# Norm sums between the groups of a projection, and one pass over x at the entry to a second network

## The reference

```
# first network, per layer l (cut)
u = rms_norm(x, g_mix[l]) * (1 + sc_a) + sh_a          # "stat_mix": mean of x*x
...
x = x + gt_a * (merged @ w_out[l])                     # "w_out0".."w_out7"
u = rms_norm(x, g_ffn[l]) * (1 + sc_f) + sh_f          # "stat_ffn"
h = silu(u @ w_ffn_gate[l]) * (u @ w_ffn_up[l])
x = x + gt_f * (h @ w_ffn_down[l])                     # "down0".."down7"
# after two layers
x = rms_norm(x, g_final)                               # "norm0"
# second network, first layer
h_lat = modulate(rmsnorm(x,   norm_g[0, 0]), sh1, sc1)     # "norm1", both together
h_ctx = modulate(rmsnorm(ctx, norm_g[0, 0]), csh1, csc1)
```

## Time and profile before

| | |
|---|---|
| median of 3 runs | 2476.86 us (2463.89 to 2481.15) |
| the profiled execution | 2472.51 us, its span 2470.7 us |
| TensorE busy | 2227.5 us, 90% of the span |
| DVE busy | 1634.2 us, 66% |
| ACT busy | 1174.1 us, 48% |
| mean granted TensorE clock | 0.949 of 2.4 GHz |
| matmuls of the sums, L913 and L1064 | 84 records, 144 records |

### The profile page before, as it was taken

One profiled execution on the slowest core, in us unless ns is written; L12 is line 12 of the kernel. 1 busy time (PEld: TensorE's weight loads), 2 busy tenths in 40 slices (PEclk: granted clock), 3 DMA queues, 4 the chain that ended last, 5 costly groups with the idle time before them and its releaser, 6 DMA issues.

```text
span 2470.7 us, 36391 instructions
## 1 busy us (share of the span) xinstructions
PE 2227.5 (90%) x13724; PEld 1945.1 (79%) x13724; DVE 1634.2 (66%) x2617; ACT 1174.1 (48%) x2021; POOL 32.4 (1%) x18
## 2 busy tenths in 40 slices
PE   1899988999899998999786989989998899898998
PEld 0897778999897788999575566768775788888998
DVE  5557766984458776984477588938584723575983
ACT  3345563563445564563434634435253324644772
POOL 4000000000000000000000000000000000000000
PEclk8899998999899998999898999989999899998999
DMA  6456633865456633865352063535351323313553
GB/s 257 137 179 235 211 101 120 263 231 180 136 178 235 210 111 120 268 226 182 117 178 104 3 202 128 179 106 183 121 179 60 128 94 111 103 52 128 187 179 113
DMA packets 107181, 385.08 MB, mean 156 GB/s; under 512 B 11664, under 2 KB 16272, under 8 KB 105744
## 3 DMA queue, kind: packets, MB, share of 16 engines
q1 hardware_dynamic: 75680, 272.66, 32.8%
q10 hardware_dynamic: 31344, 110.24, 12.8%
HBM read 381.81 MB, written 1.05 MB: 155 GB/s over the span
## 4 chain that ended last, share of the span: by engine, by line
PE 70%; DVE 15%; DMA 6%; ACT 5%; issue 3%; ACTq 1%; DVEq 0%; SPq 0%
PE ps L863 18%; PE ps L867 18%; PE ps L866 18%; DVE ada_junk L1776 6%; DMA ring<-tape_in 3%; DMA work<-adas_in 3%; PE ps L880 3%; PE ps L884 3%; PE ps L883 3%; DVE ring_l L1751 2%; PE ps L1064 1%; PE ps L1199 1%; DVE part L1751 1%; ACT ring_r L1240 1%; PE ps L1149 1%
## 5 line engine op out<-in xcount | busy, mean ns | idle before, releaser
L863 PE MATMUL ps<-part,ring_l 128*128 128x256 f32 (+1 forms) x3808 | 1188.1, 312 | 100.2 <-DVE part L1861 39.1
L867 PE MATMUL ps<-part,ring_r 128*128 128x256 f32 (+1 forms) x3808 | 1171.5, 308 | 0.0
L866 PE MATMUL ps<-part,ring_r 128*128 128x256 f32 (+1 forms) x3808 | 1170.6, 307 | 0.0
L863 PEld LDWEIGHTS ps<-part,ring_l 128*128 128x128 f32 x3808 | 731.5, 192 | 163.1 <-issue 73.7
L1240 ACT ACTIVATE ring_r<-ring 128x1024 fp32r<-128x1024 f32 x511 | 535.4, 1057 | 633.3 <-DMA ring<-tape_in 520.3
L1751 DVE TENSOR_TENSOR ring_l<-ring,ring_r 128x1024 fp32r<-128x1024 f32 x511 | 616.0, 1220 | 221.8 <-ACT ring_r L1240 219.4
L866 PEld LDWEIGHTS ps<-part,ring_r 128*128 128x128 f32 x3808 | 733.8, 193 | 31.6
L867 PEld LDWEIGHTS ps<-part,ring_r 128*128 128x128 f32 x3808 | 731.7, 192 | 33.1
L1776 DVE SCALAR_TENSOR_TENSOR ada_junk<-work 128x1024 bf16<-128x1024 f32 x272 | 345.6, 1270 | 45.6 <-DMA work<-adas_in 30.1
L880 PE MATMUL ps<-ring_l,part 128*128 128x512 f32 x264 | 106.1, 402 | 11.0 <-ACT work L1588 6.2
L883 PE MATMUL ps<-ring_r,part 128*128 128x512 f32 x264 | 105.9, 401 | 0.0
(11 more groups left out here) (198 smaller groups left out, 1798.0 us busy)
## 6 DMA issues: line engine op xcount, KB each, us to landing
ring<-tape_in SPq DMA_DIRECT2D x518, 512.0 KB, 3.4
work<-adas_in ACTq DMA_DIRECT2D x176, 512.0 KB, 4.3
work<-ada_first_in ACTq DMA_DIRECT2D x8, 1024.0 KB, 16.2
work<-bias_in ACTq DMA_DIRECT2D x1, 2048.0 KB, 9.8
work<-cond_in ACTq DMA_DIRECT2D x1, 1536.0 KB, 8.0
x<-x_t_in ACTq DMA_DIRECT2D x1, 1024.0 KB, 12.8
x<-ctx_in ACTq DMA_DIRECT2D x1, 1024.0 KB, 5.6
x<-dist_in ACTq DMA_DIRECT2D x1, 1024.0 KB, 7.4
```

The lines of the kernel that those rows point to most:

```text
L863: mm = pe.matmul(dst, lhsT=wl, rhs=mr, start=(k == 0), stop=False)
L866: pe.matmul(dst, lhsT=wr, rhs=mr, start=False, stop=False)
L867: mm = pe.matmul(dst, lhsT=wr, rhs=ml, start=False, stop=(k == len(moving) - 1))
```

## The change

1. In the first network the squares and sums of stat_ffn are taken tile by tile: ACT squares tile k once DVE has made it, and TensorE's sum matmul for tile k stands behind group k + 2 of w_out. So five of the eight stand between groups, three behind the last. The same is done with stat_mix of layer 1 between the down groups of layer 0. ACT's rounding for the last group (`finished("w_out7")`, `finished("down7")`) moves behind the logarithm and exponential.
2. In the last layer the down groups carry the sums for the second network. ACT squares each tile twice, as x² and as (g·x)² with g = g_final, and TensorE sums both in one matmul of 512 columns (`stat_last`). The context is loaded in the feed-forward stage of that layer, squared ahead of the down groups and summed behind down1 (`stat_ctx`).
3. The scale of norm1 for `x` is worked out from these sums without a pass over the normed `x`: with s = mean x² + eps, DVE multiplies 1/s by the sum of (g·x)² (`lat_power`), and ACT takes logarithm and exponential again ("norm1x"). Norm0's scaling of `x` (`final`) is interleaved with norm1's scaling on DVE, two tiles ahead.
4. The modulation and gains of the second network's first norm are made before the down groups.

```diff
@@ TensorE, first network
+                def stat_part(k):
+                    dst = bank("stat_mix")[:, 0:T]
+                    pe.wait_ge(*squared(k, l + 1))
+                    mm = pe.matmul(dst, lhsT=const("ones"), rhs=sq[:, k, :], start=(k == 0), stop=(k == KD - 1))
...
+                def stat_last(k):
+                    pe.wait_ge(*squared2(KD + k))
+                    mm = pe.matmul(bank2("norm0"), lhsT=const("ones"), rhs=SQ_OF[0][:, k, :, :].rearrange("p a t -> p (a t)"),
+                                   start=(k == 0), stop=(k == KD - 1))
...
                 for f in range(KD):
                     project(f"w_out{f}", pairs(mix_r, mix_l, KD), (lambda k: mix_made(k, l)) if f == 0 else None)
-                stat("stat_ffn", [(squared, KD + k, sq[:, k, :]) for k in range(KD)])
+                    if f >= LAG:
+                        stat_mixed(f - LAG)
+                for f in range(KD - LAG, KD):
+                    stat_mixed(f)
...
                 for f in range(KD):
                     project(f"down{f}", pairs(hidden_r, hidden_l, FT), (lambda k: hidden_made(k, l)) if f == 0 else None)
+                    if l == DEPTH - 1 and f == 1:
+                        for k in range(KD):
+                            stat_ctx(k)
+                    if f >= LAG:
+                        (stat_part if l < DEPTH - 1 else stat_last)(f - LAG)
+                for f in range(KD - LAG, KD):
+                    (stat_part if l < DEPTH - 1 else stat_last)(f)
...
-            stat2("norm0", squared2, 0, SQ_OF[0], T)
-            stat2("norm1", squared2, 1, SQ_OF[1], T2)
@@ ACT
                 for k in range(KD):
-                    finished(f"w_out{k}")
                     act.wait_ge(*x_mixed(k, l))
                     act.activation(sq[:, k, :], xt[:, k, :], ACT.Square).then_inc(squared.sem, 1)
-                inverse_rms(3, "stat_ffn", D)
+                    if k < KD - 1:
+                        finished(f"w_out{k}")
+                inverse_rms(3, "stat_ffn", D, l)
+                finished(f"w_out{KD - 1}")
                 shifted(1, 3)
...
+                    if l == DEPTH - 1 and f == FT // 2:
+                        act.wait_ge(*u_made(2 * KD - 1, l))
+                        act.dma_start(x[:, :, T:T2], ctx_in).then_inc(loaded["ctx"], 16)
...
+                    for f in range(KD):
+                        act.wait_ge(*x_ready(f, DEPTH))
+                        act.activation(SQ_OF[0][:, f, 0, :], xt[:, f, :], ACT.Square)
+                        act.activation(SQ_OF[0][:, f, 1, :], xt[:, f, :], ACT.Square,
+                                       scale=misc_of("g_final")[:, f:f + 1]).then_inc(squared2.sem, 1)
+                        if f < KD - 1:
+                            finished(f"down{f}")
...
+                    act.wait_ge(*done2("norm0"))
+                    act.activation(lat_log, bank2("norm0")[:, 0:T], ACT.Ln, scale=1.0 / D, bias=const("eps")).then_inc(log_mean2.sem, 1)
+                    act.wait_ge(*log_mean2(ROOT["norm0"]))
+                    act.activation(lat_inv, lat_log, ACT.Exp, scale=-1.0).then_inc(rstd2_made.sem, 1)
+                    act.activation(lat_rstd, lat_log, ACT.Exp, scale=-0.5).then_inc(rstd2_made.sem, 1)
+                    act.wait_ge(*lat_power(0))
+                    act.activation(rstd2[:, 0:T], lat_inv, ACT.Ln, scale=1.0 / D, bias=const("eps")).then_inc(log_mean2.sem, 1)
+                    act.wait_ge(*log_mean2(ROOT["norm1x"]))
+                    act.activation(rstd2[:, 0:T], rstd2[:, 0:T], ACT.Exp, scale=-0.5).then_inc(rstd2_made.sem, 1)
+                    finished(f"down{KD - 1}")
...
             act.wait_ge(*x_ready(KD - 1, DEPTH))
-            act.dma_start(x[:, :, T:T2], ctx_in).then_inc(loaded["ctx"], 16)
             act.dma_start(na_bias, bias_in).then_inc(loaded["na"], 16)
...
-            norm_in(0, lambda k: x_ready(k, DEPTH), None)
-            act.wait_ge(loaded["ctx"], 16)
-            norm_in(1, lambda k: scaled2(k), 0)
+            shifted2(1, 0)
@@ DVE, entry to the second network
+            dve.wait_ge(*rstd2_made(ROOT_MADE["norm0"]))
+            dve.tensor_tensor(lat_inv, lat_inv, bank2("norm0")[:, T:T2], ALU.mult).then_inc(lat_power.sem, 1)
+            dve.wait_ge(*rstd2_made(ROOT_MADE["norm0_root"]))
+            for k in range(LAG):
+                final(k)
+            dve.wait_ge(loaded["ctx"], 16)
             norm_in(1, 0, 0)
```

More of the change, by code:

```diff
@@ L312, in ffn @@
         return o + [f"post{1 + 2 * j}"]
-    o = ["norm0", "norm1"] + [f"sgu_g{b}" for b in range(4)] + [f"na_qk{f}" for f in range(2 * WT)]
+    o = ["norm1", "norm0"] + [f"sgu_g{b}" for b in range(4)] + [f"na_qk{f}" for f in range(2 * WT)]
     o += [f"sgu_u{f}" for f in range(WT)] + [f"mix{t}" for t in range(WT)] + [f"na_v{b}" for b in range(4)]
@@ L764, in bank2 @@
         def bank2(name):
-            return ps[:, GROUP2[name] % BANKS]
+            return ps[:, {"norm0": STAT_BANK, "norm1": CTX_BANK}.get(name, GROUP2[name] % BANKS)]
         def done2(name):
@@ L1309, in load_ada @@
                         .then_inc(ada_landed[t % ADA_SLOTS], 16)
[L1311 to L1314 removed]
+                if l == 0:
+                    for k in range(KD):
+                        act.wait_ge(*x_ready(k))
+                        act.activation(sq[:, k, :], xt[:, k, :], ACT.Square).then_inc(squared.sem, 1)
+                    inverse_rms(0, "stat_mix", D, l)
                 shifted(0, 0)
@@ L1820, in _, with modulation2, gain2 @@
             dve.wait_ge(*ada_early(ADA_EARLY - 1))
+            def modulation2(j, first, last, n):
+                dve.tensor_tensor(mod[:, first:last, :], ada_sums[:, first:last, :],
+                                  par2_of(j, "b_ada", first, last - first).unsqueeze(2).to_broadcast([P, last - first, 2]), ALU.add)\
+                    .then_inc(mod2_made.sem, 1)
+                dve.wait_ge(*mod2_made(10 * j + n))
+            def gain2(j, n, last):
+                chunk = (1, 2, 4, 5)[n]
+                for c in range(2):
+                    m, g = mod[:, chunk * KD:(chunk + 1) * KD, c], par2_of(j, "norm_g", n * KD, KD)
+                    if n % 2 == 0:
+                        a = dve.scalar_tensor_tensor(gains[:, n, c, :], m, 1.0, g, ALU.add, ALU.mult)
+                    else:
+                        a = dve.tensor_tensor(gains[:, n, c, :], m, g, ALU.mult)
+                    a.then_inc(mod2_made.sem, 1)
+                dve.wait_ge(*mod2_made(10 * j + last))
             for l in range(DEPTH):
```

126 lines of the change are left out of this document (78 added, 48 removed).

## The result

| | before | after |
|---|---|---|
| median, us (lowest to highest) | 2472.77, 5 runs (2463.89 to 2481.15) | 2447.57, 5 runs (2442.78 to 2450.98) |
| ratio, 95% interval | | 0.9892 (0.9862 to 0.9923) |
| the profiled execution, its span, mean clock | 2472.51, 2470.7, 0.949 | 2442.78, 2441.0, 0.956 |

The kernel became faster by 25.2 us, 1.1%. The interval is clear of no change, but it reaches to either side of 1%. Forecast were 17.0 us and a time of 2460; the measured time lies just inside the lower end of the range, 2447.

What follows compares the result with a forecast made beforehand. TensorE, busy nine tenths of the span, loses time in four gaps set by chains over ACT, PE and DVE. Gains of 0.7 + 0.7 + 5.1 + 10.5 = 17.0 us gave a median of 2460, range 2447 to 2473 (8 in 10).

Steps and rivals of the forecast that it cites:

- Behind it ACT has the three roundings: Entry to the second network: ACT does three roundings, then five DMA issues (2.9 us), so the first shift starts at 1189.3.
- so it waits for ACT: Entry: DVE finishes three `final` and six scalings at 1188.3, before ACT's first shift at 1189.3, so DVE waits.
- its upper bound, 13: Entry: upper bound of the 10.5 us gain, 13 us, if the issues overlap the roundings; lower bound 8.
- The 1.0 us for the clock: Entry: longer idle means 1.7 to 2.7 us more at half clock, costing 1.0 us of the 11.5 raw gain.
- the layers: Between the layers, down7 to the next projection: gap 6.8 us in place of 14.0, gain 5.1 us, bounds 3.5 and 7.6.
- w_out: End of w_out in both layers: gap 5.3 us in place of 8.2, gain 0.7 us twice, bounds 0 and 1.5.
- Given back: Second network's first projection: the 10.5 us entry gain goes into the 8.2 us wait for split panels; 2470.4 us, chance 0.11.
- Starved ring: Down groups: ACT rounds panels too late and each of 14 groups stalls; at 3 us each 2502 us, chance 0.04.
- Not doing what it says: Down: ACT's order keeps squares behind a panel's landing, so 5.1 us falls to 3.5; within the bounds, no separate chance.
- Slack and phase: Shorter idles keep the clock up, or later attention stages start in another clock phase, by 8 us or more; 2451, chance 0.09.
- The sum: All four places: 0.7 + 0.7 + 5.1 + 10.5 = 17.0 us gain, bounds 11.5 and 23.6.
- The cover of 2 us: Second network: mask panel ready at 1207.6, needed by TensorE's 73rd matmul at 1209.6; cover 2 us where it was 3.4.

Runs made afterwards that it cites:

- rounds_behind: The changed kernel with the three roundings for down7 of the last layer behind the shifts of norm1: 2446.80 us, ratio 0.9905 to the kernel before.
- issues_behind: The changed kernel with the five DMA issues of the entry to the second network behind the shifts of norm1: 2457.20 us, ratio 0.9944 to the kernel before.
- null: The kernel before, unchanged, run again: 2469.71 us, ratio 1.0008 to the kernel before.
- down_only: The kernel before with only stat_mix of layer 1 put between the down groups of layer 0: 2463.72 us, ratio 0.9978.
- wout_only: The kernel before with only the sums of stat_ffn put between the w_out groups, in both layers: 2465.28 us, ratio 0.9987.
- sums_behind: The changed kernel with all eight sums of each norm behind the last group again, squares still tile by tile: 2448.98 us, ratio 0.9925 to the kernel before.
- full: The changed kernel measured again, against the kernel before on the same chip: 2448.73 us against 2467.68, ratio 0.9903.
- better: The changed kernel with last-group roundings behind the shifts at all four places and table and weight issues moved earlier: 2446.06 us, ratio 0.9893 to the kernel before.

## Why the prediction was right and wrong

**What failed is the size of one term, and the step is this:** "Behind it ACT has the three roundings, 1184.55 to the start of the third at 1186.45 (a DMA issue starts with the last rounding, as now), and five DMA issues": the first shift was put 9.65 us behind the end of down7. It starts 7.98 us behind it. The two timelines show why. Before, on ACT:

```profile
1173.60 1.06 ACT L1240 ACTIVATE ring_r<-ring 128x1024 fp32r<-128x1024 f32 x1 [0.41 <-DMA ring<-tape_in]
1176.30 1.06 ACT L1240 ACTIVATE ring_r<-ring 128x1024 fp32r<-128x1024 f32 x1 [1.64 <-DMA ring<-tape_in]
1176.31 0.58 ACTq L1553 DMA_DIRECT2D x<-ctx_in  x1
```

The first issue started with the last rounding because that rounding had waited 1.64 us for its panel, and the issues with it. After the change all three panels are there, nothing in that row waits, and the issuing side of ACT runs ahead: its first issue starts at 1170.09, before the first rounding at 1170.27. What stood as a sum is a maximum: rounds_behind and issues_behind each left the first shift where it was within 0.3 us, and the forecast's order would have moved it by 2.8 and 2.9. The Trainium skill (Perfetto Trace Analysis, DVE / Act Engine Instruction) has the sequencer push such an instruction into a wait queue, from which it goes to an execution FIFO, and turn to the next one. That agrees with 1170.09 against 1170.27; that the first issue in the kernel before started only with the rounding that had waited for its panel (1176.31 against 1176.30) doesn't follow from it, and the runs show it all the same. With the step fell "so it waits for ACT": DVE's nine operations end at 8.92 us (8.65 was forecast), when the shifts are there. The gap is 9.95 us in place of 11.65, and the raw gain 30.9 - 9.95 - 7.8 = 13.1 in place of 11.5. The prediction had this as its upper bound, 13, "the issues overlap the roundings".

**The 1.0 us for the clock** was not paid in this pair: 3.0 us at half clock behind 7.2 us of idle, against 3.4 behind 4.8. The prediction had the idle itself too long, 9.1 for 7.2, as TensorE has its last sum at 1167.88. Twelve executions bear on the rest. By the granted clock, TensorE ran at half clock behind its start for 3.4, 3.4, 3.4 and 4.2 us with the 4.8 us idle (before, null, down_only, wout_only), and for 3.0, 3.5, 3.7, 4.5, 5.1, 5.2, 5.4 and 5.9 us with the 7.2 us idle (the eight traces that have it). The means are 3.6 and 4.5; at half clock the difference is worth 0.4 us, and it is smaller than the spread. My reading of a longer slow stretch from a longer idle was drawn from two rows and doesn't hold as an exact rule. The Trainium skill (TensorE: Matmul & The Clock Gate, The HAM clock gate) says that the slow start varies from run to run with phase. The traces agree that it varies, behind the same 7.2 us of idle from 3.0 to 5.9 us; what it varies with they don't show.

**Right: the layers**, 6.75 us against 6.8, gain 5.15 (14.0 - 6.75 - 2.1) against 5.1. Right also, a little low or high, w_out: gaps 5.62 and 5.41 us where 5.3 was said; 8.16 and 8.31 before, so 0.4 and 0.8 gained against 0.7 twice. What held tile 7's square there in layer 0 was DVE, late with its fold, and the prediction had ACT's rounding alone. The end of down moved by 2.1 and 7.8 us against 2.1 and 7.7. Between the layers the reason was right too: it counted the eight squares, the roundings with their wait and the half clock as what goes, and said of the moved sums only that they were in the gap already. sums_behind bears it out: with all of those gone and the sums back in their old place the gain stays. How the 13 us of the entry divide between the second pass over `x` that is gone and the squares that moved, no run separates.

**Refuted rivals.** *Given back:* the wait of 8.2 us is 8.0 to 8.2 in every kernel after the change. *Starved ring:* TensorE has no wait in w_out and down but 0.83, 0.38 and 0.16 us for the squares of tile 7, and at the start of w_out0 waits of up to 1.65 us that the kernel before has too. *Not doing what it says:* ACT's order is as it said. *Slack and phase* named 2451, and the first result, 25.2 us, was of its size. But the largest part of the 10.5 us in same code lay ahead of the change, where no shorter idle can have brought it about, and on the second occasion the medians kept none of it. A gain of a few us outside the places is not excluded by medians with such intervals; nothing shows one.

**The sum:** 0.4 + 0.8 + 5.15 + 13.1 = 19.4 us against 17.0, as full measured 19.0. The other 6 us of the 25.2 are the spread of a median, which the range had at "about 6 us": luck, as the prediction itself called it. That the change came to 1.1% and not within 1%, as was forecast at 0.82, rests on both: 2.4 us of mis-sized terms and the 6 us. On the second occasion the ratio is 0.9903, with an interval to either side of 1%. (The upper end of the range is 2 us too high by its own terms: 2476.9 - 11.5 + 6 is 2471.)

**The cover of 2 us** for the bias table held: TensorE comes to its 73rd matmul 18.2 us behind its start (18.3 was said), and the panel is ready at 16.1. In issues_behind the cover was 3.4, as the slow start there was 2.5 us longer; it also shows the price if the cover goes.

## What to carry to other kernels

In this kernel the sums on TensorE needed no place between groups. What paid is that their inputs were ready, so that they neither waited nor ran in the slow clock, and between the layers, by another 2.0 us in better, that roundings for a later stage stood behind the chain and not ahead of it. Where a chain over several engines sets a gap, write out each engine's own row to the end: here ACT's and DVE's ended within 0.1 us of one another, and an edit on either gained nothing, while both together gained 1.2 us. For a change of 1% compare stretches of the same code in both traces before believing the difference of two medians.

## What the runs showed of the hardware that was not expected

DMA issues in ACT's stream ran beside its ACTIVATEs: five issues (2.98 us from first to last) beside three roundings (2.93 us), both over within 0.13 us of one another. Taking the issues away moved ACT's next instruction by 0.01 us (7.75 against 7.76), taking the roundings away by 0.3, and taking both away by 1.3 us. In the kernel before, the squares stood behind the six issues in ACT's program and had to wait for them, 2.42 us, and in rounds_behind the first shift stood 2.46 us for five. So here an issue ran beside the ACTIVATEs that stand ahead of it, and held up those behind it. It didn't start ahead of one that still waited for its semaphore: in the kernel before, the first issue came 0.01 us behind the start of the rounding that had waited 1.64 us, long after the fold that the issue itself waits for.

Sums issued without idle ran at full clock (eight in 3.62 us, L923 in sums_behind), the same sums after 4.84 us of idle took 6.13 us.

The same kernel on one core varied by 22 us, 0.9%, over 35 runs. In the profiled executions of before and after the first 389 us are the same code, and the granted clock in one stretch of 55 us is 0.84 in the one and 0.91 in the other.
